# A hybrid decoder layer: sample attention in eight portions inside the attention stage, next weights prepared at its end, one sum moved to TensorE

## What is computed

```python
xn = rmsnorm(x, norm_w); z = xn @ w_in
q, k, v, g_attn, u, g_ssm = jnp.split(z, cuts, axis=-1)
q = rope(rmsnorm(q, q_norm_w), pos); k = rope(rmsnorm(k, k_norm_w), pos)
...
s = einsum(q, [previous block's k, own k]) / sqrt(64); p = sink_softmax(s, mask, sinks); o = p @ v
...
x_t = lam * x_(t-1) + Bbar u_t;  y = Re(C x) + D u
...
a = rmsnorm(attn_o * silu(g_attn)); g = gelu(ssm_y); s = g * sigmoid(g @ w_glu + b_glu)
s = rmsnorm(s * silu(g_ssm)); out = x + concat([a, s]) @ w_out
```

## Time and profile before

| | us |
|---|---|
| median of 3 runs | 1922.61 (1922.33 to 1923.34) |
| profiled execution, device time | 1921.25 |
| its span in the profile | 1919.4 |
| TensorE matmul busy | 1758.0 (92%) |
| VectorE (DVE) busy | 1384.1 (72%) |
| ScalarE (ACT) busy | 677.3 (35%) |
| GpSimd (POOL) busy | 533.4 (28%) |

### The profile page before, as it was taken

One profiled execution on the slowest core, in us unless ns is written; L12 is line 12 of the kernel. 1 busy time (PEld: TensorE's weight loads), 2 busy tenths in 40 slices (PEclk: granted clock), 3 DMA queues, 4 the chain that ended last, 5 costly groups with the idle time before them and its releaser, 6 DMA issues. The chain is left out here.

```text
span 1919.4 us, 26075 instructions
## 1 busy us (share of the span) xinstructions
PE 1758.0 (92%) x8731; PEld 1418.5 (74%) x8731; DVE 1384.1 (72%) x3049; ACT 677.3 (35%) x1743; POOL 533.4 (28%) x615
## 2 busy tenths in 40 slices
PE   5899999999999983799999995888868999999999
PEld 4777777777777762688888884666656788888886
DVE  5787887888787874488889945999957456655532
ACT  5444544554454443222223202444424222222210
POOL 1122122222222210322223305889932111111110
PEclk9999999999999995799999997999989999999999
DMA  7112212211211104333143124655447535445331
GB/s 245 54 59 76 70 59 67 78 59 59 86 58 47 42 15 160 81 85 130 60 120 129 50 80 130 153 146 147 119 97 154 144 127 140 127 119 139 108 113 63
DMA packets 200485, 191.69 MB, mean 100 GB/s; under 512 B 121504, under 2 KB 159520, under 8 KB 200352
## 3 DMA queue, kind: packets, MB, share of 16 engines
q1 hardware_dynamic: 191136, 181.63, 31.8%
q10 hardware_dynamic: 9216, 8.39, 2.3%
HBM read 130.88 MB, written 59.10 MB: 99 GB/s over the span
## 5 line engine op out<-in xcount | busy, mean ns | idle before, releaser
L788 PE MATMUL ps_b<-b_WH,b_XH 128*128 128x512 f32 (+1 forms) x792 | 294.8, 372 | 19.4 <-POOL b_XL L748 11.5
L790 PE MATMUL ps_b<-b_WH,b_XL 128*128 128x512 f32 (+1 forms) x792 | 285.1, 360 | 0.0
L789 PE MATMUL ps_b<-b_WL,b_XH 128*128 128x512 f32 (+1 forms) x792 | 285.1, 360 | 0.0
L490 PE MATMUL ps_e<-e_XH,e_WH 128*128 128x464 f32 x576 | 219.9, 382 | 3.4 <-POOL e_ONES L453 3.4
L492 PE MATMUL ps_e<-e_XH,e_WL 128*128 128x464 f32 x576 | 215.7, 375 | 0.0
L491 PE MATMUL ps_e<-e_XL,e_WH 128*128 128x464 f32 x576 | 215.2, 374 | 0.0
L788 PEld LDWEIGHTS ps_b<-b_WH,b_XH 128*128 128x128 f32 x792 | 150.8, 190 | 53.8 <-issue 23.2
L748 POOL TENSOR_TENSOR b_XL<-b_XT,b_XH 128x1024 fp32r<-128x1024 f32 x33 | 79.5, 2410 | 370.1 <-ACT b_XH L908 370.1
L790 PEld LDWEIGHTS ps_b<-b_WH,b_XL 128*128 128x128 f32 x792 | 150.7, 190 | 24.2
L789 PEld LDWEIGHTS ps_b<-b_WL,b_XH 128*128 128x128 f32 x792 | 151.1, 191 | 21.2
L974 ACT ACTIVATE b_SM<-ps_b,b_small 128x128 f32<-128x128 f32 x256 | 113.7, 454 | 110.2 <-DVE b_small L1111 107.6
(11 more groups left out here) (334 smaller groups left out, 3894.6 us busy)
## 6 DMA issues: line engine op xcount, KB each, us to landing
b_XT<-in_xb SPq DMA_DIRECT2D x33, 512.0 KB, 4.0
b_XR<-in_x SPq DMA_DIRECT2D x33, 512.0 KB, 5.1
e_XT<-in_xt SPq DMA_DIRECT2D x36, 464.0 KB, 3.7
l_X<-in_xr SPq DMA_DIRECT2D x32, 512.0 KB, 4.4
out_out<-l_OUT SPq DMA_DIRECT2D x32, 512.0 KB, 3.0
scr_gs<-e_TG SPq DMA_DIRECT2D x36, 232.0 KB, 2.0
scr_u<-e_UT SPq DMA_DIRECT2D x12, 696.0 KB, 3.3
g_U<-scr_u SPq DMA_DIRECT2D x192, 43.5 KB
```

The costliest lines, as they stand in the source:

```text
L490: pe.matmul(bank(s, m), WH[:, k, cols], XH[s % 2][:, k, :], start=(k == 0), stop=False)
L788: pe.matmul(bank[:, 0:c1 - c0], XH[b][:, k, :], WH[:, k, c0:c1], start=(k == 0), stop=False)
L789: pe.matmul(bank[:, 0:c1 - c0], XH[b][:, k, :], WL[:, k, c0:c1], start=False, stop=False)
L790: mm = pe.matmul(bank[:, 0:c1 - c0], XL[b][:, k, :], WH[:, k, c0:c1], start=False, stop=(k == KD - 1))
```

## The change

- **Sample attention** is no block of its own. Its steps stand inside the attention stage's loops as samples(t), for t = 4 (transposes of q and k), 5 and 6 (scores), 7 (maxima), 8 (exponentials), 9 (normalisation), 10 and 11 (transposes of the probabilities), 12 (gate), 13 (values), 14 (squares), 15 (their total). Eight of these write the PSUM bank TB on PE, which q_transposes(t+1) also writes, and so it waits for their readers. On PE samples(t) stands behind scores(t), on ACT behind exps(t), on DVE ahead of split_probs(t). The cached keys come transposed from the host; the square sum of the samples goes to RAO's common chain, and the transposes back and the final normalisation fall away.
- **The next block's weights** (8 pieces): five are loaded in the SyncE queue's turn 17, its first input in turn 19; ACT and DVE split five pieces and the input at tile 32 and behind it, POOL takes three of the four low parts of the input; pieces 5 to 7 are loaded at the end and split at the start of early_projections. RAO's chain stands in strip 4 there.
- **Nine staging buffers** for the attention stage's weights; all input pieces come ahead of the squares in the queue and on ACT.
- **State space:** the sum WT is gone from DVE. PE multiplies both halves of WB with the identity and accumulates: four matmuls in place of two transposes.
- The blocks' large tensors share three areas of SBUF.

```diff
+    def load(self, sp, I, k):
+        if k >= self.STAGED:
+            sp.wait_ge(self.lo, k - self.STAGED + 1)
+        sp.dma_start(self.staged(k), I["w_in"][k * P:(k + 1) * P, C_U:C_U + 2 * DS]).then_inc(self.ld[k % self.STAGED], 16)
+
+    def high(self, act, k):
+        act.wait_ge(self.ld[k % self.STAGED], 16 * (k // self.STAGED + 1))
+        act.activation(self.weights("H", k), self.staged(k), ACT.Copy, scale=self.NW[:, k:k + 1]).then_inc(self.hi, 1)
+
+    def low(self, dve, k):
+        dve.wait_ge(self.hi, k + 1)
+        dve.scalar_tensor_tensor(out=self.weights("L", k), in0=self.staged(k), scalar=self.NW[:, k:k + 1],
+                                 in1=self.weights("H", k).bitcast(F32), op0=ALU.mult, op1=ALU.subtract).then_inc(self.lo, 1)
...
+                for k in range(shared.STAGED, KD):
+                    shared.high(act, k)
                 for p in range(NPC):
...
-                        pe.matmul(bank(s, m), WH[:, k, cols], XH[s % 2][:, k, :], start=(k == 0), stop=False)
-                        pe.matmul(bank(s, m), WH[:, k, cols], XL[s % 2][:, k, :], start=False, stop=False)
-                        mm = pe.matmul(bank(s, m), WL[:, k, cols], XH[s % 2][:, k, :], start=False, stop=(k == KD - 1))
+                        if m == 0 and s == 0:
+                            pe.wait_ge(shared.lo, k + 1)
+                        high, low = (shared.weights(hl, k)[:, cols] for hl in "HL")
+                        pe.matmul(bank(s, m), high, XH[s % 2][:, k, :], start=(k == 0), stop=False)
...
+                for k in range(shared.STAGED, KD):
+                    shared.low(dve, k)
+                dve.wait_ge(shared.lo, KD)
...
+                    if s == 4:
+                        dve.scalar_tensor_tensor(out=VA[:], in0=SA[:], scalar=0.25 / DA, in1=EPSX[:], op0=ALU.mult, op1=ALU.add).then_inc(va, 1)
+                        dve.wait_ge(va, 1)
+                        rsqrt_chain(dve, ra, Tile(None, 0), RAO[:], VA[:], SA[:], YA[:], 1.0, 0.0)
...
+        TAKEN = (QK_AT,) + SCORES_AT + (CACHED_AT, NEW_AT, GATE_AT, VALUES_AT, TOTAL_AT)
+
...
                 load_xt(0)
-                load_w(2)
-                load_w(3)
+                for n in range(KD):
+                    load_w(n)
                 for dst, src in ((WN, I["qk_norm"]), (TAKE, I["take"]), (HALF, I["halves"]), (FIRST, I["first"]), (SINK, I["sinks"]), (ID, I["ident"])):
                     sp.dma_start(dst[:], src).then_inc(const_ld, 16)
                 load_xr(0)
-                load_xr(1)
                 load_rope(0)
-                for n in range(4, KD):
-                    load_w(n)
+                load_w(KD)
+                load_w(KD + 1)
                 load_xt(1)
                 load_rope(1)
-                for n in range(KD, 2 * KD):
+                load_xr(1)
+                for n in range(KD + 2, 2 * KD):
                     load_w(n)
-                    if n - KD < 3:
-                        load_xr(n - KD + 2)
+                for t in range(2, 5):
+                    load_xr(t)
...
+                    if t == TOTAL_AT + 2:
+                        sp.wait_ge(s_full, taken(TOTAL_AT))
+                        for k in range(shared.STAGED):
+                            shared.load(sp, I, k)
...
+                for k in range(shared.STAGED, KD):
+                    shared.load(sp, I, k)
...
+                    pool.tensor_tensor(pieces(NX["L"], p), pieces(shared.XT, p), pieces(NX["H"], p).bitcast(F32), ALU.subtract)
...
+                    elif t in SCORES_AT:
+                        g = SCORES_AT.index(t)
+                        pe.wait_ge(s_ld, 64)
+                        pe.wait_ge(s_out, taken(t - 1))
+                        for quad in range(2):
+                            for bi in range(4):
+                                b = 4 * quad + bi
+                                q_ = QT0[group(g), b, :, :].rearrange("p j t -> p (j t)")
+                                o = TB[32 * bi:32 * bi + 32, quad * NK:(quad + 1) * NK]
+                                pe.matmul(o[:, 0:P], q_, CKT[group(g), b, :], start=True, stop=True)
+                                mm = pe.matmul(o[:, P:NK], q_, KT0[group(g), :], start=True, stop=True)
+                        mm.then_inc(s_full, 1)
...
+                    elif t == VALUES_AT:
+                        pe.wait_ge(s_out, taken(t - 1))
+                        pe.wait_ge(kept_v, 1)
+                        for b in range(B):
+                            for g in range(NKV):
+                                i, c = 2 * g + b // 4, slice(32 * (b % 4), 32 * (b % 4) + 32)
+                                o = TB[group(g), 32 * b:32 * b + 32]
+                                pe.matmul(o, CV[:, b, group(g)], PTC[:, i, c], start=True, stop=False)
+                                mm = pe.matmul(o, V0[0:NSAMP, group(g)], PTN[0:NSAMP, i, c], start=False, stop=True)
+                        mm.then_inc(s_full, 1)
...
+                    if taken(t - 1):
+                        pe.wait_ge(s_out, taken(t - 1))
...
+                    elif t == EXP_AT:
+                        act.wait_ge(s_max, 4)
+                        for i in range(4):
+                            act.activation(S[:, i, :], S[:, i, :], ACT.Exp, bias=S_NM[:, i:i + 1], accum_out=S_SUM[:, i:i + 1]).then_inc(s_exped, 1)
+                        act.activation(S_ES, S_SD, ACT.Exp).then_inc(s_exped, 1)
...
-                high_w(0)
-                high_w(1)
                 high_x(0)
-                for n in range(2, KD):
+                for n in range(KD + 2):
                     high_w(n)
                 square_x(0)
-                square_x(1)
                 high_x(1)
-                for n in range(KD, 2 * KD):
+                for n in range(KD + 2, 2 * KD):
                     high_w(n)
-                    if n - KD < 3:
-                        square_x(n - KD + 2)
+                for t in range(1, 5):
+                    square_x(t)
...
+                    if t == NT - 1:
+                        act.wait_ge(ga_full, NT)
+                        shared.high(act, 0)
+                        next_high_x(0)
+                        shared.high(act, 1)
                     if t:
                         exps(t)
+                        samples(t)
                     if t + 1 < NT:
...
+                next_high_x(1)
+                shared.high(act, 2)
+                shared.high(act, 3)
+                next_high_x(2)
+                shared.high(act, 4)
+                next_high_x(3)
...
+                        for quad in range(2):
+                            ins = dve.scalar_tensor_tensor(out=S[:, 2 * g + quad, :], in0=TB[:, quad * NK:(quad + 1) * NK], scalar=SCALE,
+                                                           in1=SMASK[:, quad, :], op0=ALU.mult, op1=ALU.add)
+                        ins.then_inc(s_out, 1)
...
+                    elif t == NORM_AT:
+                        dve.wait_ge(s_exped, 5)
+                        dve.tensor_tensor(S_DEN, S_SUM, S_ES, ALU.add).then_inc(s_probs, 1)
+                        dve.wait_ge(s_probs, 1)
+                        dve.reciprocal(S_RD, S_DEN).then_inc(s_probs, 1)
+                        dve.wait_ge(s_probs, 2)
+                        for i in range(4):
+                            dve.tensor_scalar(S[:, i, :], S[:, i, :], S_RD[:, i:i + 1], None, ALU.mult).then_inc(s_probs, 1)
...
+                    if t == NT - 1:
+                        for k in range(3):
+                            shared.low(dve, k)
...
-                dve.wait_ge(a_out, NT - 1)
...
+                dve.wait_ge(nx_hi, 4)
+                dve.tensor_tensor(pieces(NX["L"], 3), pieces(shared.XT, 3), pieces(NX["H"], 3).bitcast(F32), ALU.subtract)
+                for k in range(3, shared.STAGED):
+                    shared.low(dve, k)
...
-                    wt.wait(pe, tile(t))
+                    pe.wait_ge(w_parts, t + 1)
                     if t:
                         pe.wait_ge(o2_out, t)
                     for a in range(2):
-                        pe.transpose(psWO[:, P * a:P * a + P], WT[t % RT][:, 8 * a:8 * a + 8, :].rearrange("p t h -> p (t h)"), SWAP[:, 0, :])
+                        for i in range(2):
+                            pe.matmul(psWO[:, P * a:P * a + P], WB[t % RT][:, i, 8 * a:8 * a + 8, :].rearrange("p t h -> p (t h)"), SWAP[:, 0, :],
+                                      start=(i == 0), stop=(i == 1))
...
-                    wt.link(dve, tile(t), dve.tensor_tensor(WB[:], y_, back, ALU.mult))
                     if t >= RT:
                         mats.wait(dve, tile(t - RT))
-                    wt.link(dve, tile(t), dve.tensor_tensor(WT[t % RT][:], WB[:, 0], WB[:, 1], ALU.add))
+                    dve.tensor_tensor(WB[t % RT][:], y_, back, ALU.mult).then_inc(w_parts, 1)
```

More of the change, by code:

```diff
@@ L138, with __init__ @@
 class Discretize:
-    def __init__(self, ctx, sem, nc, I):
+    def __init__(self, ctx, sem, nc, I, shared):
```

(14 more changed lines are left out.)

418 lines of the change are left out of this document (177 added, 241 removed).

## The result

| | before | after |
|---|---|---|
| median, us | 1922.47 (1920.85 to 1923.34, 4 runs) | 1879.92 (1879.25 to 1882.34, 4 runs) |
| ratio, 95% interval | | 0.9782 [0.9765, 0.9799] |
| profiled execution, us; its span | 1921.25; 1919.4 | 1879.85; 1878.0 |

The account below looks back on a forecast made before the run. TensorE was taken to set the pace of two thirds, the change touching three stretches where it doesn't. -52.7 + 13 - 7 + 3.5 - 11.5 = -54.7 from 1921.25 gives 1866.6, say 1867; range 1850 to 1882, narrower 1859 to 1875.

Parts of the forecast that it names:

- Sample stage, -52.7: Between attention and early projections: the separate sample stage goes, saving 52.7 us, with attention's end unchanged within 3 us.
- Portions, +13: Attention stage: the sample steps placed in tiles 4 to 15 add 13 us, bounds 8 and 18.
- The start, -7: Kernel start: nine staging buffers shorten weight loading and everything behind shifts, saving 7 us, between 3 and 9.
- by ACT's order they end near 29.5: Kernel start: the five squares x_rsqrt(0) needs end near 29.5 us, so DVE starts then what started at 37.17.
- Early projections, +3.5: Start of early projections: ACT splits pieces 5 to 7 ahead of the first squares, delaying total(0), costing 3.5 us.
- State space, -11.5: State-space stage: taking WT from DVE saves 0.65 us in some 18 groups, 11.5 in all; bounds 17 and 3.
- CB inherits the wait: State-space groups: CB issues in WT's place against the same POOL instruction and takes over its wait; WT's waiting is 0.96.
- the second (1877): Attention and start: portions cost more, 18 us, and the start gives only 2, making 1877; chance 0.17.
- The first: State-space stage: CB meets no long POOL instruction and groups come down to PE's 7.0, -6 us, 1861; chance 0.17.
- The third: State-space stage: identity matmuls cost four transposes each, 2.2 us a group, +10 instead of -11.5, 1888; chance 0.03.
- The fourth, the clock: Attention stage: PE waits in five tiles lower the granted clock, some 15 us a tile, 1942 with five; chance 0.02.
- The fifth: Attention's end: something doesn't work as said, POOL and DVE hold each other, block ends 6 us later, 1873; chance 0.05.

Follow-up runs that it names:

- experiment 5: Changed kernel with the sample values by fewer calls, the new values multiplied with 128 columns at once and the cached products added: 1872.03 us.
- experiment 3: Changed kernel with VectorE's portions placed behind split_probs instead of ahead of it: 1880.08 us.
- experiment 4: Changed kernel with ScalarE's four sample exponentials moved from ahead of copy_q to behind the squares of the inputs: 1878.54 us.
- experiment 2: Changed kernel with four staging buffers for the attention weights instead of nine: 1893.05 us.
- experiment 8: Changed kernel with square 1 ahead of six high parts, q and k copies ahead of squares 3 and 4, first rotation before the inputs' rsqrt: 1877.60 us.
- experiment 6: Changed kernel with the sample values in two portions, in tiles 13 and 14, instead of one: 1877.45 us.
- experiment 11: Changed kernel with merged values, later exponentials, new start order, two end-of-attention moves, later totals, and VectorE's maxima and normalisation behind the previous tile's gate_attn: 1850.74 us.

## Why the prediction was right, and where it was wrong

- **Sample stage, -52.7, end unchanged within 3.** Right, with the end at +2.8 at the edge of its bound. Both costs were named, POOL holding the last softmax (1.4, "1 to 2") and the store behind the loads. What wasn't seen is that the low parts of the weights and POOL's third part meet as well (5.56 for three instead of 3.9).
- **Portions, +13.** 19.7, outside the bounds of 8 to 18. Two steps failed. The first is the values in tile 13, "5.6 at full clock, may overlap, 4.5": a call at the lower clock (0.35) was halved with the clock, and full clock makes it 0.23 and not 0.175, so 7.4; the halves didn't overlap (in experiment 5 they did; which of its two differences did it stays open); and the clock fell, 3.0 more. The second is the DVE portions "0.35 each", priced at their length in a stage where POOL stood still. In tiles 7, 8 and 9 they, or the rotation they pushed, met POOL's low part: 10.0 instead of the 4.65 forecast. Tiles 4, 10, 11, 12 and 15 cost 0.3 together instead of 2.2: four transposes and ACT's copy added nothing that the tiles' lengths show. The meetings are shown by experiments 3 and 4; how much of the 10.0 is DVE's time and how much the late q is not separated.
- The rule for it was at hand. The prediction cites the Trainium skill (SBUF — State Buffer, "Who interferes with whom") for the state-space stage, and the rows above agree with it, the scaling of one SBUF input (L1375) included, which the same section lists among those that can take the shared port. It was not asked of the attention stage, where a tile before had no such meeting: every portion placed there moves DVE against POOL.
- **The start, -7.** -3.4, in the bounds of 3 to 9. The step "by ACT's order they end near 29.5" failed: it took the inputs as there when ACT comes to them, and the loads of the last two wait in the queue for squares that stand behind six weights. The last ended near 33.4. Experiments 2 and 8 show both sides of it.
- **Early projections, +3.5.** 5.3: the wait for total(0) is 5.45 (forecast 6.5, before 2.99), which is 2.5 of it. Most of the other 2.8 is the clock: the first product takes 8.0 us instead of 6.9, and behind the wait the granted clock is 0.64 from 761 to 765 and 0.51 from 765 to 769, which costs 1.2 more than the same place before. The term was of a wait alone; a wait of this length also costs what follows.
- **State space, -11.5.** -13.1. The mechanism and the size of a group (7.3; 7.36) are right, but not the step "CB inherits the wait": CB waits only 0.22 more. The wait went to WB (1.05 instead of 0.69) and Z's sum (1.03 instead of 0.58). Counted by DVE's starts, the first nine groups give 2.1 and the next 19 give 11.9, 0.6 each; 0.8 of these 14.0 isn't in the ledger's stretch, because PE's first matmul comes that much sooner behind DVE's first group. The last three groups are 2.8 shorter on DVE and give nothing: PE ends 39.7 us behind the start of the first of them, before 39.5. So the forecast of 7.0 for PE's own work was right (7.06), and so was that it would be the bound where DVE's groups are shorter.
- **Rivals.** Nearest was the second (1877), portions dearer and start smaller: it had the sums right and the price of a hand-over wrong. The first did not come: PE's group is 7.06 and DVE's stays at 7.36. The third fell: the four matmuls take 0.99 us and not 2.2. The fourth, the clock, happened: in tile 13 for 7 us, behind small calls in a row and not behind PE waits, and in tile 8 for 3 us, behind a wait of 2.43. Its counter, "PE waits of 3 us in this stage leave the clock at 1.00", was misread: the longest single wait between 50 and 706 us of the kernel before is 1.6. The fifth came by half: the end is 2.8 longer and not 6.
- **The number.** That it lies in the range owes something to the range's width. The errors of the terms add up to 13.3 us, and experiments 3, 4 and 6 show that the largest of them, the portions', was not one of size alone.

## What to carry to other kernels

Work put into a full stage costs no more than its length only if nothing moves against its neighbours on a shared resource: for each place, write down what GpSimd does at that moment, and put VectorE's SBUF work where VectorE waits or beside its PSUM instructions. A wait that goes can come back two stages on, so follow the producer's chain (here load, square, sum) and ask who needs the value at all: moving the totals behind more products won 9 us where moving one of them won nothing. And count what frees the buffer of the last load before placing a store behind it.

## What the runs showed of the hardware

- A VectorE maximum of two SBUF operands of 128x4 elements, 0.16 us with GpSimd idle (experiment 11), takes 2.29 when a GpSimd instruction of 2.40 started 0.13 us ahead of it: its size didn't bound its wait.
- The granted clock fell to the lower level in a row of fp32 calls of 32 columns (from 328.7, after 5.5 us of them), with TensorE without a wait since 320.6; with half as many in a row it stayed at 1.00.
- Fp32 calls of 32 columns follow each other every 0.23 us when calls of 128 and of 64 rows on the same columns alternate, and every 0.07 when all have 128 rows and neighbours write the other half of the partitions.
